# An attention, expert and recurrence block on one core: an expert piece and half a gather are moved ahead, two expert pieces are loaded in halves, and the second norm's rows are loaded last

## The reference

```python
t = moba_attention(h, a_w_in[j], a_w_out[j], rel_bias)        # 8 heads, causal
h = layer_norm(DEEPNORM_ALPHA * h + t, ln_g[i, 0], ln_b[i, 0])
f = moe_ffn(h, moe_w_router[i], ...)   # 32 experts, 4 for each token
h = layer_norm(DEEPNORM_ALPHA * h + f, ln_g[i, 1], ln_b[i, 1])
```

## Time and profile before

| what | value |
|---|---|
| median of 3 runs | 1375.93 us (1375.58 to 1377.43) |
| the profiled execution | 1376.69 us, of which the span from first to last instruction 1374.9 us |
| PE busy | 1330.1 us, 97% of the span |
| DMA moved | 484.17 MB, mean 352 GB/s |
| mean granted TensorE clock | 0.994 of 2.4 GHz |

### The profile page before, as it was taken

How to read it: one execution, slowest core, us unless ns; L and a number is a source line. 1 busy time by engine, 2 the same in 40 slices (tenths; PEclk the granted TensorE clock), 3 DMA queues, 4 the chain that set the end, 5 groups by cost and what they waited for, 6 DMA issues and landing times.

```text
span 1374.9 us, 17056 instructions
## 1 busy us (share of the span) xinstructions
PE 1330.1 (97%) x7358; PEld 718.6 (52%) x7358; DVE 441.2 (32%) x746; ACT 346.9 (25%) x576; POOL 49.6 (4%) x60
## 2 busy tenths in 40 slices
PE   9999999999999999969999999999999999999997
PEld 7996333333333333323333333333336998999986
DVE  5565121112111111101211111111107776888854
ACT  4541011101101110100110101100116545666642
POOL 2010000000000000000000000000002000022200
PEclk9999999999999999989999999999999999999999
DMA  9968999999999999999999999999996444265530
GB/s 378 376 233 359 428 421 430 430 432 429 430 431 430 430 431 429 431 429 430 431 432 429 432 429 431 429 431 430 432 427 242 153 154 153 87 254 183 184 123 31
DMA packets 44378, 484.17 MB, mean 352 GB/s; under 512 B 4780, under 2 KB 4832, under 8 KB 13712
## 3 DMA queue, kind: packets, MB, share of 16 engines
q1 hardware_dynamic: 42432, 477.63, 83.4%
q0 software_dynamic: 1872, 5.44, 1.1%
HBM read 481.99 MB, written 1.06 MB: 351 GB/s over the span
## 4 chain that ended last, share of the span: by engine, by line
PE 78%; DMA 15%; DVE 4%; issue 1%; ACT 1%; DVEq 0%; SPq 0%; ACTq 0%
PE bank L835 25%; PE bank L641 19%; PE bank L843 13%; DMA ring<-in_moe_w_gate_up 12%; PE bank L1143 4%; PE bank L855 3%; PE bank L808 3%; PE bank L624 3%; DMA ring<-in_w_in 2%; PE bank L827 2%; PE bank L751 2%; PE bank L1079 1%; PE bank L1029 1%; DMA arena<-in_x_by_feature 1%; DVE w_split L1552 1%
## 5 line engine op out<-in xcount | busy, mean ns | idle before, releaser
L835 PE MATMUL bank<-ring,arena 128*64 128x512 f32 x2048 | 448.9, 594 | 9.8 <-DMA ring<-in_moe_w_gate_up 9.8
L835 PEld LDWEIGHTS bank<-ring,arena 128*64 128x64 f32 x2048 | 143.2, 137 | 313.2 <-issue 290.3
L1750 DVE TENSOR_SCALAR arena<-bank 128x512 f32<-128x512 f32 x32 | 22.1, 692 | 654.8 <-PE bank L835 654.7
L843 PE MATMUL bank<-ring,arena 128*64 128x512 f32 x1008 | 223.5, 595 | 1.8 <-DMA ring<-in_moe_w_down 1.3
L641 PE MATMUL bank<-x_hi,w_split 128*128 128x256 f32 x1056 | 195.2, 285 | 2.1 <-DVE x_lo L1559 2.1
L641 PEld LDWEIGHTS bank<-x_hi,w_split 128*128 128x128 f32 x1056 | 167.2, 193 | 2.6 <-DVE x_lo L1559 1.5
L1552 DVE TENSOR_TENSOR w_split<-ring,w_split 128x2048 fp32r<-128x2048 f32 x61 | 139.5, 2289 | 60.4 <-ACT w_split L1198 60.2
L641 PE MATMUL bank<-x_lo,w_split 128*128 128x256 f32 x528 | 150.1, 284 | 0.0
L1299 ACT ACTIVATE arena<-arena 128x512 f32<-128x512 f32 x32 | 20.2, 630 | 495.3 <-DVE arena L1750 495.3
L843 PEld LDWEIGHTS bank<-ring,arena 128*64 128x64 f32 x1008 | 69.8, 137 | 135.3 <-issue 126.4
L1198 ACT CAST w_split<-ring 128x2048 fp32r<-128x2048 f32 x62 | 118.2, 1910 | 74.2 <-PE bank L641 42.5
(11 more groups left out here) (288 smaller groups left out, 1102.1 us busy)
## 6 DMA issues: line engine op xcount, KB each, us to landing
ring<-in_moe_w_gate_up SPq DMA_DIRECT2D x128, 2048.0 KB, 34.5
ring<-in_moe_w_down SPq DMA_DIRECT2D x63, 2048.0 KB, 34.1
ring<-in_ffn_w_up SPq DMA_DIRECT2D x22, 1024.0 KB, 4.8
ring<-in_w_in SPq DMA_DIRECT2D x14, 1024.0 KB, 8.0
ring<-in_ffn_w_down SPq DMA_DIRECT2D x11, 1024.0 KB, 4.9
ring<-in_a_w_in SPq DMA_DIRECT2D x10, 1024.0 KB, 20.9
ring<-in_a_w_out SPq DMA_DIRECT2D x2, 2048.0 KB, 14.0
ring<-in_w_out SPq DMA_DIRECT2D x4, 1024.0 KB, 5.0
```

The source lines that it names most:

```text
L835: last = mm(bank[q // 2][half * 64:half * 64 + 64, :], chunk(xeT, c), w[:, c % 2, q * 512:(q + 1) * 512], start=False, stop=c == KC - 1)
L843: last = mm(bank[3][half * 64:half * 64 + 64, :], chunk(actT, c), w[:, c % 4, half * 512:(half + 1) * 512], start=c == 0, stop=c == KC - 1)
```

## The change

- Piece 10 is loaded as soon as the attention's last value product is done (`o_ps`), ahead of the `OUT_ORDER` loop. For this the first norm's rows move out of its place, to floats 13612 and 6144 of the arena, and the first of them is loaded right after the attention's bias, the second just before the router's weights.
- Piece 11 is loaded in two halves of 1 MB: the first when PE has done the first of the two chunks of piece 0 (`first_chunk`), the second when piece 0 is done.
- The first norm's last operation is split in column halves, and PE turns each half as it comes. The ranks of tile 0 are made before the logits of tile 1, and the selection and the gather of expert 0 are made tile by tile (`first_places`, `gather_first`). The bias of expert 0 is added between the two tiles' logits (so the last output bank is 7 and no longer 0), and the tables are made behind piece 0 of `gate_up`. Shorter matmuls (`fill`) take the place of some of `repeat`.
- The last piece (191) is loaded and used in two halves. Scatter of tile 1 and the turn of the gates move between the two last down pieces.
- The second norm's rows are loaded by SP behind piece 191 and ahead of the second block's weights, and no longer by POOL in expert 1.
- On ACT, the copy of the last result goes ahead of `split_hi(IN2)`, and the table load for the norm goes ahead of both.

```diff
-        OUT_BANKS = (4, 6, 5, 0)
+        OUT_BANKS = (4, 6, 5, 7)
+        row_g0, row_b0 = at(13612, D), at(6144, D)
...
+            sp.wait_ge(o_ps, PAIRS)
+            load_piece(SPARE)
             for k, q in enumerate(OUT_ORDER):
...
-            sp.wait_ge(h1_ready, NT)
-            load_piece(SPARE)
-            for n in range(SPARE + 1, first_late):
+            sp.wait_ge(first_chunk, 1)
+            load_half(HALVED[0], 0)
+            sp.wait_ge(*freed(HALVED[0]))
+            load_half(HALVED[0], 1)
+            for n in range(SPARE + 2, first_late):
...
+            sp.wait_ge(*freed(HALVED[1]))
+            for j in range(2):
+                load_half(HALVED[1], j)
+            sp.dma_start(row_g, row(ln_g[1, :], D)).then_inc(ln1_in, 16)
+            sp.dma_start(row_b, row(ln_b[1, :], D)).then_inc(ln1_in, 16)
...
-            pool.wait_ge(max_ready, H)
-            pool.dma_start(row_g, row(ln_g[0, :], D)).then_inc(ln0_in, 16)
-            pool.dma_start(row_b, row(ln_b[0, :], D)).then_inc(ln0_in, 16)
+            pool.dma_start(row_g0, row(ln_g[0, :], D)).then_inc(rel_in, 16)
             pool.wait_ge(pt_ps, H)
             pool.wait_ge(o_ps, PAIRS)
+            pool.dma_start(row_b0, row(ln_b[0, :], D)).then_inc(ln0_in, 16)
             pool.dma_start(wr, w_router.rearrange("(c p) e -> p c e", p=P)).then_inc(moe_small_in, 16)
...
             pool.dma_start(bdown, b_down[:, :]).then_inc(moe_small_in, 16)
-            pool.dma_start(row_g, row(ln_g[1, :], D)).then_inc(ln1_in, 16)
-            pool.dma_start(row_b, row(ln_b[1, :], D)).then_inc(ln1_in, 16)
...
             for t in range(NT):
-                pe.wait_ge(h1_ready, t + 1)
                 for g in range(2):
+                    pe.wait_ge(h1_ready, 2 * t + g + 1)
...
                 if t:
+                    pe.wait_ge(chosen_ready, 1)
+                    mm(RANKS[0], before, chosen[:, 0, :], start=True, stop=True).then_inc(rank_ps, 1)
+                    pe.wait_ge(h1T_dve, 1)
...
                 if t == 0:
+                    pe.wait_ge(bsel_ready, 1)
+                    add_bias()
                     repeat(3, 1)
...
+            pe.wait_ge(sel_ready, 1)
+            gather_first(0)
+            mm(RANKS[1], ones, chosen[:, 0, :], start=True, stop=False)
+            fill()
             pe.wait_ge(chosen_ready, 2)
+            mm(RANKS[1], before, chosen[:, 1, :], start=False, stop=True).then_inc(rank_ps, 1)
+            fill()
+            pe.wait_ge(sel_ready, 2)
+            gather_first(1).then_inc(xe_ps, 1)
+            fill()
...
-            pe.wait_ge(sel_ready, 1)
-            gather().then_inc(xe_ps, 1)
...
             pe.wait_ge(xe_ready, 1)
             turn_chunks(2, xe, 2).then_inc(xeT_ps, 1)
+            fill()
...
+                    if n == HALVED[1]:
+                        scatter(1)
+                        pe.wait_ge(selg_ready, i + 1)
+                        turn_gates().then_inc(selgT_ps, 1)
+                        pe.wait_ge(*arrived(n))
+                        down_e(s, buffer_of(n, 4), (0, 1))
+                        pe.wait_ge(last_half_in, 32)
+                        down_e(s, buffer_of(n, 4), (2, 3)).then_inc(piece_done, 1)
...
+                    if n == 0:
+                        gate_up(s, buffer_of(n, 2), (0,)).then_inc(first_chunk, 1)
+                        gate_up(s, buffer_of(n, 2), (1,)).then_inc(piece_done, 1)
+                        tables()
...
                 if i == LAST:
-                    split_hi(IN2)
+                    nc.scalar.preload_act_table_set(log_exp)
                 if i != LAST - 1:
                     take_items(i)
+                if i == LAST:
+                    split_hi(IN2)
...
-                stt(h1[:, t, :], h1[:, t, :], r, row_b, ALU.mult, ALU.add).then_inc(h1_ready, 1)
+                dve.wait_ge(ln0_in, 16)
+                for g in range(2):
+                    cols = slice(g * 512, (g + 1) * 512)
+                    stt(h1[:, t, cols], h1[:, t, cols], r, row_b0[:, cols], ALU.mult, ALU.add).then_inc(h1_ready, 1)
...
             choose(0)
             dve.wait_ge(h1T_ps, 4)
             dve.tensor_copy(h1T[:, 4:8, P:T], bank[7][:, :].rearrange("p (c n) -> p c n", c=4)).then_inc(h1T_dve, 1)
+            first_places(0)
             choose(1)
             dve.wait_ge(chosen_ready, 2)
+            first_places(1)
```

More of the change, by code:

```diff
@@ L775, in _, with add_bias, gather_first, fill @@
             before = const("before")
+            def add_bias():
+                for half in range(2):
+                    for q in range(2):
+                        rows = slice((half * 2 + q) * 32, (half * 2 + q) * 32 + 32)
+                        mm(bank[q][half * 64:half * 64 + 64, :], bias_sel[rows, :], bgu[rows, :],
+                           start=True, stop=False)
+            def gather_first(t):
+                for half in range(2):
+                    last = mm(bank[2][half * 64:half * 64 + 64, :], sel[:, t, :], h1[:, t, half * 512:(half + 1) * 512],
+                              start=t == 0, stop=t == NT - 1)
+                return last
+            def fill():
+                mm(bank[3][:, 0:T], ident, cst[:, 0:T], start=True, stop=True)
             for t in range(NT):
-                pe.wait_ge(h1_ready, t + 1)
                 for g in range(2):
+                    pe.wait_ge(h1_ready, 2 * t + g + 1)
                     b = 4 + 2 * t + g
@@ L821, in chunk, with gate_up @@
                 return v[:, c % 4, (c // 4) * 64:(c // 4) * 64 + 64]
-            def add_bias():
-                for half in range(2):
-                    for q in range(2):
-                        rows = slice((half * 2 + q) * 32, (half * 2 + q) * 32 + 32)
-                        mm(bank[q][half * 64:half * 64 + 64, :], bias_sel[rows, :], bgu[rows, :],
-                           start=True, stop=False)
-            def gate_up(s, w):
-                for c in (2 * s, 2 * s + 1):
+            def gate_up(s, w, chunks=(0, 1)):
+                for c in (2 * s + k for k in chunks):
                     for q in range(4):
@@ L857, in scatter, with tables @@
                 return last
-            pe.wait_ge(sel_ready, 1)
-            gather().then_inc(xe_ps, 1)
-            pe.wait_ge(gates_ready, 1)
-            for t in range(NT):
-                turn(bank[3][0:N_EXP, t * P:(t + 1) * P], gates[:, t, :])
-            for t in range(NT):
-                turn(bank[3][0:N_EXP, T + t * P:T + (t + 1) * P], place[:, t, :])
-            for t in range(NT):
-                last = mm(bank[4][0:N_EXP, 0:1], chosen[:, t, :], ones[:, 0:1], start=t == 0, stop=t == NT - 1)
-            last.then_inc(table_ps, 1)
             pe.wait_ge(xe_ready, 1)
             turn_chunks(2, xe, 2).then_inc(xeT_ps, 1)
+            fill()
+            def tables():
+                pe.wait_ge(gates_ready, 1)
+                for t in range(NT):
+                    turn(bank[3][0:N_EXP, t * P:(t + 1) * P], gates[:, t, :])
+                for t in range(NT):
+                    turn(bank[3][0:N_EXP, T + t * P:T + (t + 1) * P], place[:, t, :])
+                for t in range(NT):
+                    last = mm(bank[4][0:N_EXP, 0:1], chosen[:, t, :], ones[:, 0:1], start=t == 0, stop=t == NT - 1)
+                last.then_inc(table_ps, 1)
             def put_down(i):
@@ L928, in _ @@
                     pe.wait_ge(y_ready, LAST)
-                    for t in range(NT):
-                        scatter(t)
+                    scatter(0)
                 if i + 1 < N_EXP and not pause:
@@ L1667, in choose, with select_bias @@
                                   ALU.add).then_inc(chosen_ready, 1)
+            def select_bias(i):
+                ts(bias_sel, ones[:, 0:CAP], const("own")[:, i:i + 1], None, ALU.mult).then_inc(bsel_ready, 1)
+            select_bias(0)
             for t in range(NT):
```

81 lines of the change are left out of this document (42 added, 39 removed).

## The result

The changed kernel takes 1385.77 us (median of 5 runs, 1382.87 to 1388.42), the kernel before 1375.58 beside it: ratio 1.0071, 95% interval 1.0055 to 1.0088. By this ratio it is slower by 9.8 us (the medians differ by 10.2), where the prediction said 1372.5, 3.4 us faster. The profiled execution took 1387.83, with a span of 1386.0.

The account below looks back on a forecast made before the run. The bound was the unbroken stream of weight loads up to piece 189, plus 13.7 us of PE work. Gains of 3.3 + 0.2 - 0.1 = 3.4 us took the median from 1375.93 to 1372.5, range 1370.0 to 1374.6.

Parts of the forecast that it names:

- the third rival: Router: POOL's small gate-up bias loads starve behind the second row and beside piece 10, making the kernel slower; chance 0.05.
- The router: Router on PE: half gather, bias moved and shorter filler, less a loss, start the first gate-up 1.35 us earlier, at 130.9.
- The tables: Behind piece 0 of gate-up: no longer hidden, they cost 0.76 us in full, 0.9 at most, 0.6 at least.
- Piece 10 early: Before the router: issued at 100.25, its load fills a DMA hole; queued stream ends some 4 us earlier, but the lead doesn't last.
- piece 20 has landed by 186: Expert 1's weight stream: piece 20 is in by 186, so the engines idle for 3 us before piece 21 lands.
- Piece 21: End of expert 1: held by its place in the ring, issued at 185.9 and landing 7.8 us later, at 193.7.
- the hole ahead of 188: Expert 1's weight stream: a hole in the DMA just before 188, given as a sign the forecast is right.
- Piece 22: Behind piece 21: lands at 198.6 against 201.9, a gain of 3.3 us holding both the lead and the rows that left.
- the rows: Second norm's rows: leaving expert 1 counted within the 3.3 us; ahead of the second block's weights charged 0.1, at most 0.5.
- The end: Behind piece 189: last piece's halves 0, ACT's split 0.2 us gained, the rows 0.1 lost; bounds -0.5 to +0.2.
- ScalarE's order: After the last expert: result copy no longer behind ACT's split, which waited for a load; 0.2 us gained.
- Halves: Piece 11: first half issued at 132.8, cutting costs the engines next to nothing; last piece: value 0, up to 1.8 if late.

Follow-up runs that it names:

- experiment 2: The changed kernel with piece 10 issued later, behind the loads of OUT_ORDER: 1376.11 us (10 runs), ratio 1.0002.
- experiment 4: The kernel before with only piece 10 early and the first norm's rows moved as in the change: 1382.27 us (4 runs), ratio 1.0048.
- experiment 1: The changed kernel with the four gate-up bias loads moved to right behind the first norm row, near 27 us: 1377.27 us (11 runs), ratio 1.0007.
- experiment 3: The changed kernel with six filler matmuls in place of one before PE's wait for the small loads: 1381.63 us (5 runs), ratio 1.0036.
- experiment 5: Experiment 1 with ScalarE's cast of the first w_in piece back ahead of the last take_items: 1376.35 us (10 runs), ratio 1.0008.
- experiment 7: Experiment 1 with ScalarE's order back and the second norm's rows loaded by SyncE behind the first w_in piece: 1375.87 us (10 runs), ratio 1.0001.
- experiment 8: Experiment 1 with the down biases loaded by SyncE behind piece 21 in place of by GpSimd: 1378.1 us (8 runs), ratio 1.0018.
- experiment 6: Experiment 1 with ScalarE's order back and the second norm's rows back on POOL in expert 1: 1376.67 us (10 runs), ratio 1.0018.
- experiment 11: Experiment 10 with piece 11 loaded whole in place of in halves: 1373.52 us (11 runs), ratio 0.9983.
- experiment 9: Experiment 7 with the kernel before's 512-column filler back in the router, before PE's wait for the first chosen: 1373.63 us (11 runs), ratio 0.9987.
- experiment 10: Experiment 9 with three more fillers on PE in the second norm: 1374.29 us (11 runs), ratio 0.9987.

## Why the prediction was wrong

**The step that failed** is the price and the chance of the third rival: "104.3 + 13.3 = 117.6 would cost 0.4", and "by bytes all that is queued is through by about 115. 0.05". The last bias landed at 122.1. 13.3 was one landing beside SP's stream, and it was used as if it were the worst. The four loads took 13.7 to 18.4 us beside two 2 MB pieces, issued 2 to 4 us ahead of them, and 6.8 without the second. Experiments 2 and 4 show that piece 10's early issue does it, and experiment 1 that the loss hangs on these four loads. The Trainium skill, page "DMA: Bandwidth & Descriptors", section "Queues, rings and completion order", has the queues taken in turn. The trace agrees that both are served: from 103 to 117 GpSimd's queue moves 0.92 MB beside 4.03 of SP's. But the turns don't keep small loads short, as the prediction took from them. In experiment 2 GpSimd's queue moves the same 0.93 MB from 103 to 111, beside only 1.59 of SP's; and in the changed kernel its last 0.02 MB take from 117 to 122, beside 2.03 of SP's, which had issued four more pieces from 111.49 on. So the small loads lost their time after they were issued, among the bytes of SP's pieces. A full DMA alone doesn't do it: near 10 us a load of 64 KB landed in 5.4 us with the share at 1.03. What makes the difference wasn't tried.

**The same rival lacked a term.** It said a microsecond per microsecond, and no loss to be seen under 6.2 us of lateness. It came 5.0 late and cost 9.94 at gate-up: 4.96 of wait, 6.3 of halved clock behind it (experiment 3), less 1.3 gained in the router.

**The router: right.** Predicted 1.35, measured 15.10 - 13.79 = 1.31, with the clock at 1.00. **The tables** cost what the upper bound said: from gate-up to the issue of piece 21 it takes 186.28 - 131.18 = 55.10 in place of 54.20, so all that was added there costs 0.90, and not 0.76. **Piece 10 early** does start the stream earlier, and the lead doesn't last, as said; but "piece 20 has landed by 186" was 3.5 us off, since the lead went before it. **Piece 21**: predicted 185.9 and 193.7, measured 186.28 and 194.3 (experiment 1), with the hole ahead of 188. **Piece 22 was mis-sized:** "193.7 + 4.87 = 198.6" gives 3.3 us; it landed at 200.5 to 200.8 in experiments 1, 5, 7 and 8, a gain of 1.1 to 1.4. Its time was its own issue, 190.9, plus 9.7 to 10.0 in all of them, whenever piece 21 had landed (194.1 to 195.4). The prediction gave it 7.8, the time of a load with the engines to itself. In 190 to 195 the engines move 341 to 403 GB/s, not 431, though they read as busy. And the rows cost expert 1 only 0.3 to 1.4 us (experiment 6); that most of their bytes filled the hole is likely, not shown. At the end 1.0 to 2.1 us of the 3.3 arrive (last wait 1017.4 to 1018.5 against 1019.50, in the profiles whose router kept its clock).

**The end: wrong.** ScalarE's order was booked as 0.2 gained, the rows as 0.1 lost. The cast that moved behind `take_items` started GpSimd 2.3 us later against VectorE (2.56 us ahead of the small step in place of 4.91) and cost 1.8: 17.63 to 17.89 in the changed kernel and experiments 1, 2 and 8, against 15.86 to 15.87 in 6 and 7. Each operation was priced alone; who else would run at that time wasn't asked.

**Halves**: piece 11's halves are worth nothing that reaches the end (experiment 11); the prediction gave them no term of their own. The last piece's halves weren't undone alone, nor was the tables' place.

**What stays open.** In the profiles of experiments 2 and 6 the clock falls in the router with no wait for a load ahead of it, in those of 1, 5, 7 and 8 it doesn't. With one filler of 512 columns back, three profiles of three are free of it, which four of six were without. The median falls by 2.2 us (7 against 9, each beside its own runs of before), but neither of these two profiles has the fall in the router, and their spans differ by 0.6; so it isn't shown that the filler works through the router's clock. Nor are experiment 1's slower runs explained by the router: its profile is one of them (1377.98), with the clock at 1.00 there and low in the second norm.

```profile
125.00:130.00 5.00, 4.81 (x22) 1.99 (x22) 2.73 (x14) 0.91 (x2) 0.00 (x0) 1.00 0.99 423
...
1050.00:1052.00 2.00, 1.37 (x7) 0.97 (x6) 1.79 (x5) 2.00 (x7) 1.10 (x3) 0.50 0.11 16
```

What tips the clock in a single execution isn't shown. Experiment 8's profiled execution is its fastest; seven of its eight runs have a mean clock of 0.989 to 0.993, so its median says more of the clock than of the down biases.

## What to carry to other kernels

Before a large load is moved to an earlier time, list the small loads issued by other queues near that time and who waits for them; issue those first, or well ahead. Take the spread of small-load landings from several rows, and not one of them as the worst. Price a late load twice where it stops PE: once for the wait and once for the slower clock behind it, and keep PE busy there. A stream that the ring holds gives back neither lead nor bytes in full; read from the next piece's issue and landing what its own limit is.

## What the runs showed that was not expected

- Loads of 64 KB need 6.8 us beside one 2 MB piece and 13.7 to 18.4 beside two. Issued near 28 us (experiment 1) they take 13.4 too, but nobody waits for them.
- A wait of 4.9 us was followed by half clock for most of the next 20 us; one of 4.5 (experiment 4) by half clock for the next 10. In the second norm of the kernel before PE was busy for 1.82 us of 1046 to 1050, and the clock was 0.52 in the next 2; with the fillers of experiment 10 it was busy for 3.94, and the clock 1.00. In experiments 2, 5, 6 and 8 it stayed at 1.00 without them.
- A VectorE operation of 0.21 us takes 1.98 to 1.99 when it starts under GpSimd's subtraction of 128x2048, and ends with it (the changed kernel, experiments 1, 2 and 8).
- Eleven executions of one kernel can lie in two groups 2 us apart, told from each other by the mean granted clock (experiment 1; in experiment 7 it doesn't tell them).
